# Four experts for each of 32 tokens in one gather of a hybrid decoder's expert mixer

## The chip, the core and the metric

The kernel is one program on one core of a Trainium2 chip. The metric is the time of one execution in device microseconds. Three runs of the kernel before gave 2209.43, 2210.4 and 2212.69 us; the median is 2210.4 us.

## What is computed

Two layers run over 256 prompt tokens and 8 sample tokens of width 1024. Each layer has four recurrent mixers, gates, an output projection and then the expert mixer ("PEER") that the change is about. For every token each of 8 heads picks its best 16 of 16384 experts; an expert is one row of U and one row of V. The reference, cut to that mixer:

```python
def peer_ffn(xn, w_q, keys, U, V):
    ...
    s = jnp.einsum('nhcd,hckd->nhck', q, keys.astype(jnp.float32))
    s1, i1 = lax.top_k(s[:, :, 0], PEER_TOPK)
    s2, i2 = lax.top_k(s[:, :, 1], PEER_TOPK)
    ...
    top, sel = lax.top_k(cand, PEER_TOPK)
    eidx = jnp.take_along_axis(cidx, sel, axis=-1)
    gate = jax.nn.softmax(top, axis=-1)
    ...
        hid = jax.nn.gelu(jnp.einsum('nkd,nd->nk', U[eb], xb).astype(jnp.float32), approximate=False)
        return jnp.einsum('nk,nkd->nd', (hid * gb).astype(xb.dtype), V[eb])
```

So a token has 128 experts (8 heads by 16), and its output is the sum of 128 V rows, each weighted by gelu(U row . xn) times its gate.

## The kernel before, in words

The program is written engine by engine, with semaphores set by hand; each engine works off its own list in order. The change lies in the expert mixer, the second half of each layer.

**Slots.** The 256 prompt tokens stand on the 128 partitions as two halves (tt = 0, 1). Slot s of a half is the s-th expert of every token of it: 128 slots a half, 256 for the prompt, and 8 more slots for the 8 sample tokens, which come just ahead of the last 8 prompt slots. A layer so has 264 slots. The [128, 2048] buffer of a slot holds one U row and one V row for each partition; there are 8 such buffers (`row(k)`), four in `ring` and four in `arena`.

**One slot passes five engines' queues.** GpSimd (POOL) issues an indirect DMA that fetches 128 rows of 8 KB (`fetch`, L1508 to L1517), once the buffer is free (`row_free`). VectorE (DVE) multiplies the U rows by the normalised tokens `xtok` and sums along the row (`dot`, L2076 to L2083), one value a partition. ScalarE (ACT) takes the gelu, multiplies by the gate and scales a pattern of ones to a 128x64 matrix `dg` (`gelu`, L1403 to L1408). TensorE (PE) adds the weighted V rows into PSUM (`weighted`, L1002 to L1009) with four matmuls of 64 rows by 64 columns over 512 elements each, and frees the buffer. A PE matmul in f32 shows as two records in the trace.

**Experts that aren't fetched.** 32 of the 128 first keys are chosen for a layer; the experts of these keys are computed densely by PE, so their rows get an index that is out of bounds, and the gather skips them. The dense work is spread over the slots: up products (`up_products`, L1036) beside slots 0 to 95, the one-hot gates of the dense experts (`gate_slots`, `one_hot`) beside slots 96 to 159, down products (`down_slots`, L1077 to L1091) from slot 168 on.

**Routing.** DVE finds the experts of two heads and a half at a time (`routing`, L1981 to L2064; four groups a half, eight a layer). The first group is done before the first dot, the second beside it, the others are cut into six pieces placed at fixed slots between the dots, up to slot 104. `finish` (L2039 to L2058) ends a group: the indices go to `eidx`, the gates to `gate_w`, each [128 tokens, slots].

**Loads.** The queue of SyncE (SP) loads blocks of dense experts of 512 KB each into four buffers `ub`, in order, each as soon as its buffer is free. **End of a layer.** After the last slot PE closes the sum, ACT copies it out, PE turns it and DVE adds it to the residual `x`, half a bank pair at a time (`sums_out`, `turned`, `add_turned`); then the next layer's norm begins.

## Time and profile before

| what | us |
|---|---|
| median of three runs | 2210.4 |
| the profiled execution: span from its first to its last instruction | 2214.4 |
| PE busy | 2024.7 (91%) |
| DVE busy | 1442.4 (65%) |
| ACT busy | 857.2 (39%) |
| POOL busy | 745.7 (34%) |
| PE, weighted sums (L1007), both kinds of buffer | 290.8 + 291.3 |
| DVE, dots (L2083), both kinds of buffer | 319.7 + 319.8 |

The page gives the profiled execution's span and no other time of it; it is 4.0 us above the median of the runs. "Busy" is time in which an engine executes; matmuls are pipelined, so the records of a full PE overlap. The DMA share is the mean busy share of the core's 16 DMA engines. PEclk is the granted TensorE clock, 1.00 being the upper of its two levels. An idle time stands with the engine or DMA that ended it. L numbers are lines of the kernel.

### The profile page before, as it was taken

The page shows a single profiled execution, that of the slowest core. Times are in us where ns is not written, and L with a number is a line of the kernel's source. Part 1 is how long each engine was busy: PE and PEld are TensorE (multiplying, and loading weights), DVE is VectorE, ACT ScalarE, POOL GpSimd, SP SyncE. Part 2 cuts the span into 40 slices and gives each one's busy share as a digit, 9 for nine tenths or more (in the row PEclk, how much of TensorE's full clock was granted, in tenths as well). Part 3 has the DMA queues.
Part 4 walks back from the last instruction along what each step waited for, and adds up shares of the span by engine and source line. Part 5 has one row for each costly group of instructions (what it writes and reads, how often), then busy time and mean ns, then how long its engine had stood idle before and what let it go on. Part 6 is the DMA issues. An engine that isn't in the chain of part 4 may idle for free.

```text
span 2214.4 us, 37965 instructions
## 1 busy us (share of the span) xinstructions
PE 2024.7 (91%) x13044; PEld 1237.7 (56%) x13044; DVE 1442.4 (65%) x3377; ACT 857.2 (39%) x2476; POOL 745.7 (34%) x658
## 2 busy tenths in 40 slices
PE   7999989989999888999889898899999997789997
PEld 6777668864444222454477776788544442234444
DVE  2425454589999898545533454645899989975545
ACT  2221222144545785433322213221544557853332
POOL 0400000025545676544303000000455456765442
PEclk9999889999999999999999999999999999999999
DMA  6330233568899999999843202437699999999995
GB/s 276 116 116 2 80 110 129 212 236 316 310 349 358 371 358 345 362 372 393 357 186 114 96 5 77 157 123 265 216 320 351 364 365 350 374 375 390 373 381 238
DMA packets 121546, 569.81 MB, mean 257 GB/s; under 512 B 42504, under 2 KB 44712, under 8 KB 61608
## 3 DMA queue, kind: packets, MB, share of 16 engines
q0 software_dynamic: 76032, 389.07, 46.7%
q1 hardware_dynamic: 43648, 175.12, 21.7%
q10 hardware_dynamic: 1696, 3.45, 0.4%
q8 instruction: 94, 1.54, 0.3%
q14 instruction: 76, 0.62, 0.1%
HBM read 725.63 MB, written 6.58 MB: 331 GB/s over the span
## 4 chain that ended last, share of the span: by engine, by line
PE 56%; DVE 24%; issue 10%; ACT 4%; DMA 4%; another core or an unknown queue 1%; POOL 0%; DVEq 0%; SPq 0%; ACTq 0%; POOLq 0%
PE ps L1088 12%; PE ps L1007 10%; PE ps L607 10%; PE ps L672 7%; DVE arena L2083 6%; PE ps L929 3%; PE ps L962 3%; PE ps L943 3%; DMA arena<-in_uv,arena 2%; DVE arena L2108 2%; PE ps L1036 1%; DVE arena L1978 1%; DVE arena L1969 1%; DMA ring<-in_uv,arena 1%; DVE arena L1968 1%
## 5 line engine op out<-in xcount | busy, mean ns | idle before, releaser
L1516 POOL DMA_INDIRECT arena<-in_uv,arena x264 | 332.2, 1258 | 267.6 <-PE ps L1007 214.1
L1516 POOL DMA_INDIRECT ring<-in_uv,arena x264 | 327.1, 1239 | 273.3 <-PE ps L1007 235.3
L2083 DVE SCALAR_TENSOR_TENSOR arena<-arena 128x1024 bf16<-128x1024 f32 x264 | 319.7, 1224 | 117.0 <-DMA arena<-in_uv,arena 110.5
L2083 DVE SCALAR_TENSOR_TENSOR arena<-ring,arena 128x1024 bf16<-128x1024 f32 x264 | 319.8, 1224 | 112.7 <-DMA ring<-in_uv,arena 102.2
L1007 PE MATMUL ps<-arena 64*64 64x512 f32 x2112 | 290.8, 622 | 51.0 <-ACT arena L1408 46.6
L1007 PE MATMUL ps<-ring,arena 64*64 64x512 f32 x2112 | 291.3, 623 | 45.4 <-ACT arena L1408 41.4
L1406 ACT ACTIVATE arena<-arena 128x1 f32<-128x1 f32 x528 | 105.3, 200 | 505.6 <-DVE arena L2083 499.0
L1506 POOL COPY arena<-arena 128x8 uint32 (+1 forms) x66 | 36.2, 548 | 739.2 <-DVEq L2050 738.8
L1088 PEld LDWEIGHTS ps<-hold,ub 128*128 128x128 f32 x1024 | 180.3, 189 | 161.1 <-issue 143.6
L1088 PE MATMUL ps<-hold,ub 128*128 128x256 f32 x1024 | 268.8, 398 | 0.0
L672 PE MATMUL ps<-xn,ring 128*128 128x264 f32 x1024 | 244.9, 398 | 15.1 <-remote 12.9
L672 PEld LDWEIGHTS ps<-xn,ring 128*128 128x128 f32 x1024 | 197.2, 195 | 52.2 <-issue 17.6
L1036 PEld LDWEIGHTS ps<-xn,ub 128*128 128x128 f32 x768 | 135.0, 191 | 134.6 <-issue 122.0
L1036 PE MATMUL ps<-xn,ub 128*128 128x256 f32 x768 | 207.6, 402 | 0.0
L607 PE MATMUL ps<-xn,ring 128*128 128x264 f32 x896 | 205.8, 389 | 0.0
L1408 ACT ACTIVATE arena<-const,arena 128x64 f32<-128x64 f32 x528 | 183.7, 348 | 17.2
L607 PEld LDWEIGHTS ps<-xn,ring 128*128 128x128 f32 x896 | 170.4, 191 | 33.2 <-issue 4.8
L1407 ACT ACTIVATE arena<-arena 128x1 f32<-128x1 f32 x528 | 155.6, 295 | 17.1
L1007 PEld LDWEIGHTS ps<-arena 64*64 64x64 f32 x2112 | 55.7, 132 | 140.6 <-issue 140.6
L1007 PEld LDWEIGHTS ps<-ring,arena 64*64 64x64 f32 x2112 | 56.3, 132 | 131.8 <-issue 131.7
L1190 ACT ACTIVATE arena<-ps 128x264 f32<-128x264 f32 x60 | 23.7, 395 | 206.8 <-PE ps L607 206.6
L1238 ACT ACTIVATE arena<-ps 128x264 f32<-128x264 f32 x50 | 19.3, 390 | 202.2 <-PE ps L672 201.9
(453 smaller groups left out, 2465.4 us busy)
## 6 DMA issues: line engine op xcount, KB each, us to landing
ring<-in_w SPq DMA_DIRECT2D x84, 1024.0 KB
ub<-in_uv SPq DMA_DIRECT2D x64, 512.0 KB
ub<-in_ud SPq DMA_DIRECT2D x48, 512.0 KB
hold<-in_ud SPq DMA_DIRECT2D x16, 512.0 KB, 6.4
ring<-in_uv,arena POOLq DMA_INDIRECT x264
arena<-in_uv,arena POOLq DMA_INDIRECT x264
ub<-in_w SPq DMA_DIRECT2D x4, 1024.0 KB
hold<-in_st SPq DMA_DIRECT2D x2, 2048.0 KB
```

What stands on the lines that cost most here:

```text
L607: m = mm(bank(b), w, xg[:, kt, :] if t < PLAIN_TILES else xn[:, kt, :], start=kt == 0, stop=kt == KT - 1)
L672: m = mm(bank(b), ring[:, j, at:at + P], xn[:, kt, :], start=kt == 0, stop=kt == KT - 1)
L929: m = mm(bank(b), ring[:, j, at:at + P], yy[:, 2 * m_ + k, :], start=k == 0, stop=k == 1)
L943: m = mm(bank(6 + o % 2), ring[:, j, at:at + P], src[:, kt, :], start=kt == 0, stop=kt == KT - 1)
L1007: m = mm(ps[chunk(q ^ half), SUM_BANK[tt] + half, :], dg[chunk(q), k, :], row(k)[chunk(q), D + 512 * half:D + 512 * half + 512], start=Fal ...
L1036: m = mm(bank(4 + j % 4, SEQ), u[:, kt * P:kt * P + P], xn[:, kt, 0:SEQ], start=kt == 0, stop=kt == KT - 1)
L1088: m = mm(bank(4 + dt // 2, SEQ, SEQ * (dt % 2)), ub[:, j % UB, dt * P:dt * P + P], hd[:, j, :], start=False, stop=False, skip_group_check= ...
L1406: own(act(hge[:, k:k + 1], hid[:, k:k + 1], ACT.Gelu))
L1407: own(act(hgg[:, k:k + 1], hge[:, k:k + 1], ACT.Copy, scale=gate))
L1408: act(dg[:, k, :], C("channel"), ACT.Copy, scale=hgg[:, k:k + 1]).then_inc(dg_full[k], 1)
L1516: e.indirect_dma_start(out=row(k), out_offset=None, in_=A["uv"], in_offset=bass.IndirectOffsetOnAxis(ap=ix[:, par, k:k + 1], axis=0), **sk ...
L2083: stt(prod[:, n % 2, :], u, 1.0, xtok[:, tt, :], ALU.mult, ALU.mult, accum_out=hid[:, k:k + 1]).then_inc(S("dve_hid"), 1)
```

## The change

A gather now fetches four experts for each of 32 tokens. Partition 32q + t of a slot holds expert q of token t of the group; a half is cut into four token groups g, a routing group r gives 32 slots: for each g eight, k = 0 to 7, with the ranks k and k + 8 of both heads on the four strips q. The number of slots, buffers, fetched rows and skipped rows stays.

- `dot` reads `rep[:, g]`, the 32 normalised tokens of group g written four times one below the other. SP makes these copies with 16 DMAs inside the chip for each half, 32 partitions by 4 KB each (`copies_of_rows`). `rep` and the spread indices and gates (`lay`) lie over constants that the mixer doesn't need; ACT reloads these at the end of layer 0.
- At the end of a routing group DVE spreads indices and gates with 16 copies of 32 partitions (`by_tokens`), and signals the group to POOL after them; for the first group the indices are spread and signalled first, and the gates in a second set of 16.
- `weighted` multiplies all 128 partitions by a 128x32 matrix, which sums over the four experts; four matmuls, each over 256 of the 1024 columns, go to four strips of 32 PSUM partitions.
- The first half of the second tt's sum is copied out, turned and added before the last 8 slots instead of after them; the sample sum is 256 wide instead of 1024. Loops of PE over slots are written out.

```diff
+TG = 32
+QS = P // TG
...
+        rep = const[:, OVER:OVER + QS * D].rearrange("p (a b) -> p a b", b=D)
+        lay = const[:, OVER + QS * D:OVER + QS * D + TT * 2 * SLOTS].rearrange("p (a b) -> p a b", b=2 * SLOTS)
...
-        dg = carve(SLOT, HD)
+        dg = carve(SLOT, TG)
...
+        def place(s):
+
+            tt, n = divmod(s, P)
+            return tt, n // (QS * SLOT), n // SLOT % QS
...
+                def copies_of_rows(tt):
+
+                    e.wait_ge(S("act_xt"), tt + 1)
+                    for g in range(QS):
+                        if tt:
+                            e.wait_ge(S("dve_hid"), P - (QS - 1 - g) * SLOT)
+                        if tt or g:
+                            e.wait_ge(S("sp_rep"), 16 * QS * (tt * QS + g))
+                        for q in range(QS):
+                            e.dma_start(rep[q * TG:q * TG + TG, g, :], xtok[g * TG:g * TG + TG, tt, :]).then_inc(S("sp_rep"), 16)
...
+                        if j == AHEAD[-1] + 2:
+                            copies_of_rows(0)
...
-                down_blocks(0, 12)
+                down_blocks(0, UB)
+                copies_of_rows(1)
+                down_blocks(UB, 12)
...
-                    for half in range(2):
-                        for q in range(2):
-                            m = mm(ps[chunk(q ^ half), SUM_BANK[tt] + half, :], dg[chunk(q), k, :], row(k)[chunk(q), D + 512 * half:D + 512 * half + 512],
-                                   start=False, stop=False, skip_group_check=True)
+                    for q in range(QS):
+                        m = mm(ps[TG * q:TG * q + TG, b, lo:lo + D // QS], dg[:, k, :], row(k)[:, D + D // QS * q:D + D // QS * (q + 1)],
+                               start=False, stop=False, skip_group_check=True)
...
                         if s == n - SLOT:
+                            close_sum(SUM_BANK[1])
                             e.wait_ge(S("dve_xa"), 1)
...
+                        if s == n - SLOT // 2:
+                            turned(1, 0, 3)
...
+                        sums_out(1, 2, 0)
...
+                if l + 1 < L:
+                    e.dma_start(const[:, OVER:NCONST], A["const"][:, OVER:NCONST]).then_inc(S("act_const"), 16)
+                sums_out(1, 4, 1)
...
+                def by_tokens(n, lo, hi):
+
+                    tt, r = divmod(n - 1, GROUPS)
+                    of = eg[:, tt, lo:hi, r * GH * TOPK:(r + 1) * GH * TOPK]
+                    to = lay[:, tt, :].rearrange("p (r g a k) -> p r g a k", r=GROUPS, g=QS, a=2)[:, r, :, lo:hi, :]
+                    for g in range(QS):
+                        for q in range(QS):
+                            i = e.tensor_copy(to[q * TG:q * TG + TG, g], of[g * TG:g * TG + TG, :, q * SLOT:q * SLOT + SLOT])
+                    own(i)
...
-                            e.sem_inc(S("dve_route"), 1)
+                            own(stt(to_idx, n1, layer_off[0:p1, 0:1], n2, ALU.add, ALU.add))
+                            if n == 1:
+                                by_tokens(n, 0, 1)
+                                e.sem_inc(S("dve_route"), 1)
...
+                            by_tokens(n, int(n == 1), 2)
+                        if n != 1:
                             e.sem_inc(S("dve_route"), 1)
...
-                    of = eidx[:, tt, :].bitcast(U32)
-                    ts(ix_u[:, 0, :], of, 7, 127, ALU.logical_shift_right, ALU.bitwise_and)
+                    of = ix_u[:, 1, :]
+                    own(e.tensor_copy(of, eg[:, tt, 0, :]))
+                    own(ts(ix_u[:, 0, :], of, 7, 127, ALU.logical_shift_right, ALU.bitwise_and))
...
+                    tt, r, g = place(s)
+                    if r == 0 and s % SLOT == 0:
+                        e.wait_ge(S("sp_rep"), 16 * QS * (tt * QS + g + 1))
+                    dot(s % P, rep[:, g, :], s + (SLOT if s >= samples else 0), row_round + s // SLOT)
```

The order of DVE's instructions before, where the second group's routing ends beside slots 4 and 5 (L2039 to L2058 are `finish`, L2083 is the dot):

```order
L2044 SCALAR_TENSOR_TENSOR arena<-arena 128x32
L2048 TENSOR_SCALAR arena<-arena 128x32
L2049 SCALAR_TENSOR_TENSOR arena<-arena,layer_off 128x32
L2052 TENSOR_REDUCE arena<-arena 128x2
L2053 RECIPROCAL arena<-arena 128x2
L2054 TENSOR_TENSOR arena<-arena 128x32
L2056 SCALAR_TENSOR_TENSOR arena<-arena 128x32
L2083 SCALAR_TENSOR_TENSOR arena<-arena 128x1024 x3
```

The same place now (L2025 is `by_tokens`, L2133 the dot):

```order
L2091 SCALAR_TENSOR_TENSOR arena<-arena 128x32
L2095 TENSOR_SCALAR arena<-arena 128x32
L2096 SCALAR_TENSOR_TENSOR arena<-arena,layer_off 128x32
L2101 TENSOR_REDUCE arena<-arena 128x2
L2102 RECIPROCAL arena<-arena 128x2
L2103 TENSOR_TENSOR arena<-arena 128x32
L2105 SCALAR_TENSOR_TENSOR arena<-arena 128x32
L2025 COPY const<-arena 32x16 x16
L2133 SCALAR_TENSOR_TENSOR arena<-arena,const 128x1024 x3
```

Sixteen copies stand between the end of the routing and the next dots; the other six later groups have the same, and the first group has two such rows of 32x8.

The order of PE's instructions before, in the down products (L1007 is `weighted`, L1088 a down product; the ISA rows take a semaphore):

```order
L1007 MATMUL ps<-arena 64x512 x4
L1088 MATMUL ps<-hold,ub 128x256 x3
L411 ISA
L1007 MATMUL ps<-arena 64x512 x4
L411 ISA
L1088 MATMUL ps<-hold,ub 128x256 x3
```

The same stretch now (L1039 is `weighted`, L1123 a down product):

```order
L426 ISA
L1039 MATMUL ps<-ring,arena 32x256 x4
L1123 MATMUL ps<-hold,ub 128x256
L426 ISA
L1123 MATMUL ps<-hold,ub 128x256 x2
L426 ISA
L1039 MATMUL ps<-ring,arena 32x256 x4
```

Nothing moved against the down products; the four matmuls of a slot write 32 partitions by 256 columns instead of 64 by 512.

## Rows read from the trace of the kernel before

**Rows 1.** Windows: stretch, length, busy PE, PEld, DVE, ACT, POOL; PEclk, DMA share, GB/s.

```profile
526.00:730.00 204.00, 193.69 (x1095) 92.66 (x1091) 189.62 (x549) 104.43 (x323) 106.24 (x93) 1.00 0.94 338
730.00:862.00 132.00, 107.58 (x1131) 33.05 (x1131) 124.07 (x205) 102.40 (x319) 92.77 (x75) 0.99 0.95 357
872.00:1098.00 226.00, 224.23 (x1261) 111.19 (x1257) 120.70 (x215) 81.73 (x283) 110.99 (x100) 0.99 0.98 380
1616.00:1812.00 196.00, 185.41 (x1037) 88.44 (x1035) 182.08 (x537) 98.74 (x304) 101.98 (x88) 0.99 0.94 346
1822.00:1955.00 133.00, 107.23 (x1129) 33.32 (x1125) 123.32 (x203) 101.47 (x317) 91.50 (x72) 0.99 0.97 364
1966.00:2190.00 224.00, 222.24 (x1259) 110.88 (x1260) 120.21 (x215) 81.36 (x280) 116.26 (x100) 1.00 0.98 383
```

**Rows 2.** Groups view, DVE, 488 to 730 us: busy, mean ns | idle before, what ended it.

```profile
L2083 DVE SCALAR_TENSOR_TENSOR arena<-ring,arena 128x1024 bf16<-128x1024 f32 x51 | 61.0, 1225 | 3.0 <-DMA ring<-in_uv,arena 0.8 <-DVE arena L2101 0.6 <-DVE arena L2029 0.4
L2083 DVE SCALAR_TENSOR_TENSOR arena<-arena 128x1024 bf16<-128x1024 f32 x48 | 57.2, 1225 | 1.6 <-DVE arena L2029 0.4 <-DVE arena L2101 0.3 <-issue 0.2
...
L2035 DVE TENSOR_TENSOR arena<-arena 128x1024 bf16<-128x1024 bf16 x7 | 4.8, 692 | 5.4 <-ACT arena L1365 4.6 <-issue 0.8
```

**Rows 3.** Groups view, DVE, 730 to 862 us.

```profile
L2083 DVE SCALAR_TENSOR_TENSOR arena<-arena 128x1024 bf16<-128x1024 f32 x33 | 40.1, 1219 | 1.8 <-DMA arena<-in_uv,arena 1.4 <-DVE x L2127 0.2
...
L2115 DVE TENSOR_TENSOR hold<-hold,ps 128x512 f32<-128x512 f32 x16 | 10.9, 680 | 2.8 <-remote 2.8
L2101 DVE TENSOR_TENSOR arena<-picked_f,arena 128x512 f32<-128x512 f32 x14 | 9.6, 687 | 2.0 <-ACTq L411 2.0
```

**Rows 4.** Groups view, DVE, 862 to 1098 us.

```profile
L2083 DVE SCALAR_TENSOR_TENSOR arena<-arena 128x1024 bf16<-128x1024 f32 x49 | 60.0, 1226 | 53.7 <-DMA arena<-in_uv,arena 51.6 <-issue 1.9 <-DVE arena L2054 0.2
```

**Rows 5.** Timeline, PE, second stretch: start, length, instructions in a row [idle before].

```profile
763.90 1.09 PE L1007 MATMUL ps<-ring,arena 64*64 64x512 f32 x8
764.92 0.42 PE L1071 MATMUL ps<-arena 128*32 128x128 f32 x8
765.28 0.66 PE L1060 MATMUL ps<-const,arena 128*128 128x128 f32 x4
```

**Rows 6.** Timeline, PE, third stretch.

```profile
1083.80 1.09 PE L1007 MATMUL ps<-arena 64*64 64x512 f32 x8
1084.82 1.56 PE L1088 MATMUL ps<-hold,ub 128*128 128x256 f32 x6
1086.31 1.09 PE L1007 MATMUL ps<-arena 64*64 64x512 f32 x8
```

**Rows 7.** Windows view of parts of the third stretch of both layers.

```profile
1040.00:1080.00 40.00, 40.00 (x227) 20.37 (x226) 19.45 (x33) 13.53 (x48) 22.12 (x18) 1.00 1.01 404
1060.00:1080.00 20.00, 20.00 (x115) 10.34 (x115) 8.69 (x15) 5.91 (x21) 10.85 (x9) 1.00 1.02 420
2000.00:2040.00 40.00, 40.00 (x225) 20.06 (x224) 21.13 (x35) 14.88 (x53) 22.76 (x19) 1.00 1.00 388
```

**Rows 8.** Timeline, DVE: small copies in the recurrent mixers of layer 0.

```profile
177.23 0.40 DVE L1702 COPY arena<-arena 128x16 f32<-128x16 f32 x4
...
276.35 0.17 DVE L1835 COPY arena<-arena 128x16 f32<-128x16 f32 x1
...
340.21 0.29 DVE L1884 COPY arena<-arena 128x256 f32<-128x256 f32 x1
```

**Rows 9.** Timeline, DVE: the first dot of layer 0.

```profile
486.48 1.23 DVE L2083 SCALAR_TENSOR_TENSOR arena<-ring,arena 128x1024 bf16<-128x1024 f32 x1
```

**Rows 10.** Timeline, ACT: the first half's normalised rows are put out.

```profile
473.09 1.07 ACT L1390 ACTIVATE arena<-ps 128x512 f32<-128x512 f32 x2
```

**Rows 11.** Timeline, ACT: last sums of layer 0, first root of layer 1.

```profile
1113.30 1.09 ACT L1413 ACTIVATE arena<-ps 128x512 f32<-128x512 f32 x2 [5.26 <-PE ps L1016]
...
1125.11 0.48 ACT L1157 ACTIVATE arena<-ps,const 128x264 f32<-128x264 f32 x1 [3.72 <-PE ps L580]
```

**Rows 12.** DMA issues: destination<-source, queue, count, KB, us to landing.

```profile
const<-in_const ACTq DMA_DIRECT2D x1, 2723.0 KB, 12.9
```

More of the change, by code:

```diff
@@ L1131, in _ @@
                         e.wait_ge(S("act_acc"), 4)
-                        for kt in range(KT):
-                            from_ = NS // 2 * (kt // 4)
-                            m = mm(bank(0, NS, NS * kt), xtok[:, 2, kt * P:kt * P + P], C("group")[:, from_:from_ + NS], start=True, stop=True)
+                        for half in range(2):
+                            m = e.transpose(bank(0, P, P * half), xtok[:, 2, P * half:P * half + P], C("ident"))
                         m.then_inc(S("pe_xa"), 1)
-                close_sum(1)
-                for half in range(2):
-                    turned(1, half, 5 + half)
+                close_sum(SUM_BANK[1] + 1)
+                turned(1, 1, 5)
                 e.sem_inc(arrive, 1)
@@ L2074, in _, with dot @@
                     part()
-                def dot(slot, tt, n, nth):
+                def dot(slot, rows, n, nth):
                     k = slot % SLOT
@@ L2181, in _ @@
                         e.sem_inc(S("dve_xa"), 1)
[L2182 removed]
+                    tt, r, g = place(s)
+                    if r == 0 and s % SLOT == 0:
+                        e.wait_ge(S("sp_rep"), 16 * QS * (tt * QS + g + 1))
+                    dot(s % P, rep[:, g, :], s + (SLOT if s >= samples else 0), row_round + s // SLOT)
                 own.clear()
[L2184 to L2187 removed]
+                e.wait_ge(S("pe_xa"), 4)
+                d = x[:, :, SEQ:N].rearrange("p (q h) t -> p q h t", h=2)
+                own(tt_(d, d, bank(0, 2 * P).rearrange("p (h q t) -> p q h t", h=2, t=TG)[:, :, :, 0:NS], ALU.add))
+                add_turned(1, 1, 5)
                 e.sem_inc(arrive, 1)
```

135 lines of the change are left out of this document (66 added, 69 removed).

## Prediction, made before the changed kernel ran

> **What bounds the kernel now.** I read the page for the long groups, then the stretches of the expert mixer, then what each engine waits for in them, and last the instructions of one slot. A slot is one gather of 128 rows, one dot product on VectorE (DVE), three small ScalarE (ACT) steps and one weighted sum on TensorE (PE); a layer has 264. The mixer of layer 0 falls into three stretches, that of layer 1 into the same three [rows 1]. In the first (526 to 730 us; slots 16 to 96, beside up products and the routing of later groups) DVE is busy 189.6 of 204 us, PE 193.7. In the second (730 to 862, one-hot gates) DVE is busy 124.1 of 132 and PE 107.6. In the third (872 to 1098, down products) PE is busy 224.2 of 226, DVE only 120.7, and the DMA engines' share is 0.98.
>
> Busy shares don't tell which engine is the bound; the waits do. In the first stretch the dots of DVE waited 0.8 us for a landing in 240 us [rows 2]: the rows are always there, and the stretch is as long as DVE's own chain of dots and routing. In the second it is nearly the same: 1.4 us for landings, 2.8 and 2.0 us behind PE and ACT [rows 3]. In the third one of the two groups of dots alone waited 51.6 us for landings [rows 4], because the buffers come free only as PE works through its sums. So PE's weighted sum sets the time in the third stretch only, 450 of the 2214.4 us.
>
> **PE's part.** Before, a slot is eight passes of 64x512 (four matmuls, two records each). They take 1.02 us to the next group's start, and eight passes over 128 columns, in the four column strips that the change uses, take 0.36 us (764.92 to 765.28) [rows 5]. A line through the two gives 0.36 + 128 x (0.66 / 384) = 0.58 us for eight passes over 256 columns. Bounds: half of 1.02 is 0.51, twice 0.36 is 0.72; I take 0.58, which saves 0.44 us a slot. In the first two stretches this goes into PE's idle time, since DVE is late there. In the third the slots start 2.51 us apart where six down passes stand between two sums [rows 6], 2.47 over the stretch (of its 1261 PE records 512 are down passes and some 16 others; the rest is 8 for each of 91.6 slots in 226 us); they would come to 2.03.
>
> The gathers and the down blocks would then have to come at 380 x 2.47 / 2.03 = 462 GB/s. No row has that. The busiest rows of the stretch, with a share of 0.99 to 1.01, carry 388 and 404 GB/s, and 420 in 20 us around the eight sample gathers, which skip no row [rows 7]. So what is late next is the DMA, within a few per cent of where PE stands now. I take 388, the row with a share of 1.00 and only ordinary gathers: 226 x (1 - 380/388) = 4.7 us in layer 0 and 224 x (1 - 383/388) = 2.9 in layer 1, together **-7.6**. The ends are 0 and, at 420 GB/s, -21.5 - 19.7 = -41.2.
>
> The Trainium skill, "DMA: Bandwidth & Descriptors", section "Where 436 GB/s comes from", says that for transfers from HBM the HBM side binds, at about 358 GB/s a core. By that rule the third stretch, already above it, could gain nothing, and the sum below would be 25.0 instead of 17.4 us. The rows of 388 and 404 GB/s differ from it, and the rows decide.
>
> **DVE's part.** After each group's routing the indices and gates are spread by 16 copies of 32 partitions, for the first group twice. That is 9 sets, 144 copies, in a layer. Four copies of 16 elements took 0.40 us, one alone takes 0.17 [rows 8]: (0.40 - 0.17) / 3 = 0.077 us apart, and 0.17 - 0.077 = 0.09 more for the wait at a set's end. 144 x 0.077 + 9 x 0.09 = 11.9 us. Two further copies of 128 elements before the indices are turned cost at most 0.29 each (a copy of 256 elements [rows 8]), 0.6 together. So 12.5 us a layer, **+25.0** in all. All of it is on the path: DVE has no wait for data in the first stretch that could cover it [rows 2], and the two sets of the first group stand before the first dot, which starts with no idle time of DVE before it [rows 9]. PE, ACT and the gathers queue behind it, each through the buffers. Lower end: DVE waits 4.6 us a layer for ACT before a decode [rows 2]; if copies fell fully into that, 25.0 - 9.2 = 15.8. Upper end: copies that don't overlap, 144 x 0.17 = 24.5 a layer, +50.
>
> **The copies of the normalised rows.** 32 new DMAs a layer carry 4 MB inside the chip. No row shows their time. The first 16 are issued when ACT has put out the rows at 474.2 [rows 10], behind four expert blocks on SP's queue that have been issued by then; the first four are needed by the first dot at 486.5, later still by the copies above, the next four eight slots on. SP's next block load waits behind them, for a buffer that comes free later anyway. The second 16 are needed from slot 128 and allowed from slot 104, in the second stretch: 2.1 MB at its 357 GB/s [rows 1] would be 5.9 us if nothing hid them. The DMA share of 0.95 there leaves 6.6 us of 132. I take 0; if that cover is gone, +11.7 for both layers. Against it, PE's shorter sum may end the 2.8 and 2.0 us of DVE's waits there [rows 3], -9.6 at most; I take 0 for that too.
>
> **The end of a layer.** Half of the second block's sum is now copied out and added earlier. That takes one of two ACT copies (0.55 of 1.09) and 0.68 us of DVE (one addition over 512 elements [rows 3]) from the end [rows 11], and the last sum is 0.44 shorter. But PE now stops before the fifth sample slot until all eight samples are weighed and copied out, then has four slots of down products left (8 us), which DVE's additions wait for. I take 0, with -3 to +5. The overwritten constants are reloaded behind layer 0's last gate; the first load of 2723 KB landed in 12.9 us [rows 12], and ACT reads its first constant of layer 1 some 12 us after the last copies of the sums begin [rows 11], and the reload is issued ahead of these, so 0; what lands late there is paid in full.
>
> **Sum.** 25.0 - 7.6 = +17.4 us. On the profiled execution, which has a span of 2214.4 us: 2231.8. The runs' median, 2210.4, is 4.0 below the profile, so I forecast **2227.8 us**, 0.8% slower.
>
> **Rivals.** First, the DMA speeds up once PE no longer holds the buffers: more gathers wait at the engines, and the third stretch runs at 420 GB/s. Then 25.0 - 41.2 = -16.2, **2194 us**, faster. It wins from about 404 GB/s over the whole of both third stretches, where 226 x (1 - 380/404) + 224 x (1 - 383/404) = 25.1 us pays for the copies. For it: PE is busy 40.00 of 40.00 us in the rows of 388 and 404, so PE held those rows back. Against it: a share of 0.99 to 1.01 in the same rows, and that 420 is shown only where all rows of a gather are fetched.
>
> By the same page and section of the Trainium skill the fabric allows 435 GB/s; by that figure alone the two stretches would lose 55 us. No row reaches it.
>
> Second, the gathers come less evenly. Of four tokens and all ranks of a head, rather than eight tokens and one rank, more or fewer are skipped at a time, and each dot waits for the slowest part of its gather. If the second and third stretches (132 + 226 + 133 + 224 = 715 us) become 2% longer, +14.3 in place of the gain, with half of the 11.7 for the copies: 25.0 + 14.3 + 5.9 = +45, **2256 us**. For it: DVE's 1.4 us of waiting for landings in the second stretch, at a share of 0.95, leave little room. Against it: PE gives each buffer back 0.44 us sooner.
>
> The Trainium skill's "DMA: Bandwidth & Descriptors", section "The descriptor swizzle", says that one engine serves four neighbouring partitions in each of two strips of 32. Counted so from the reference's expert indices, the fullest engine of eight gathers has 22% more rows than the mean now and 25 to 27% after. No row shows engines apart.
>
> Third, the four strips don't run side by side. Then eight passes cost 8 x 0.25 = 2.0 us (1.49 us for six passes [rows 6]), 1 us more than now, 264 us a layer less PE's idle time of some 30: about 2670 us. Rows 5 speak against it.
>
> **How the numbers follow.** Forecast 0.66, the DMA rival 0.19, the uneven gathers 0.12, strips in sequence 0.03. A measurement here can tell about 0.2% (4.4 us) from none. Faster by more: 0.15 of the first rival and 0.03 of the forecast's edge (cheap copies with 404 GB/s), 0.18. Within: 0.04 of the rival, 0.07 of the forecast, 0.11. Slower: 0.56 + 0.12 + 0.03 = 0.71. The range must reach some way to the first rival and nearly to the second: 2202 to 2252. The forecast's own range is 2215 to 2245.
>
> **What would show it.** Sixteen small copies per group on DVE, about 1.3 us each set; a first stretch longer by some 10 us with DVE still not waiting for landings; PE's eight passes at about 0.58 us and PE no longer full in the third stretch, where it waits for ACT and ACT for DVE's dots; a DMA share near 1 there at 380 to 395 GB/s. A third stretch shorter by over 12 us a layer, or copies that cost under 6 us a layer, would prove me wrong.

## The result, and the profile after

The changed kernel takes 2312.75 us (median of 4 runs, 2302.66 to 2316.96) beside 2211.55 us before (4 runs): 1.0415 times as long, 95% interval 1.0384 to 1.0447. Slower was forecast, but as 2227.8 us in a range of 2202 to 2252; the measured time is some 100 us above the one before, the forecast one was 17. The profiled execution has a span of 2313.1 us, against 2214.4.

The windows view by the same three stretches (length, busy PE, PEld, DVE, ACT, POOL, PEclk, DMA share, GB/s) is what [rows 1] became:

```profile
534.00:749.00 215.00, 172.68 (x1071) 95.56 (x1068) 200.88 (x636) 99.30 (x311) 94.16 (x90) 0.90 0.87 307
749.00:908.00 159.00, 100.42 (x1183) 48.36 (x1185) 138.25 (x234) 107.73 (x342) 102.22 (x83) 0.72 0.97 343
908.00:1124.00 216.00, 177.59 (x1180) 102.42 (x1172) 115.01 (x206) 75.46 (x270) 110.10 (x97) 0.97 0.98 381
1675.00:1889.00 214.00, 167.71 (x1065) 93.24 (x1066) 199.89 (x635) 98.92 (x310) 98.12 (x90) 0.93 0.88 314
1889.00:2052.00 163.00, 101.25 (x1188) 48.88 (x1186) 139.01 (x236) 108.29 (x343) 98.45 (x80) 0.72 0.96 341
2052.00:2270.00 218.00, 178.85 (x1180) 103.18 (x1172) 114.71 (x205) 75.00 (x268) 108.74 (x100) 0.97 0.99 386
```

PE is no longer full in the third stretch (177.6 of 216 us where it was 224.2 of 226), yet the stretch is as long as it was, and the DMA engines carry 381 and 386 GB/s where they carried 380 and 383. The first two stretches are longer. To compare kernels I cut each trace at the starts of dots: dot 0, 96, 168 and 256 of a layer (the third part so holds the eight sample slots), dot 263, the last, and VectorE's MEMSET that ends the recurrent mixers. In us, layer 0 / layer 1:

| part | before | after | grew by |
|---|---|---|---|
| MEMSET to dot 0 | 74.4 / 74.3 | 80.1 / 80.6 | 12.0 |
| dots 0 to 96 | 234.5 / 236.0 | 257.4 / 256.9 | 43.8 |
| dots 96 to 168 | 148.5 / 151.1 | 159.4 / 162.8 | 22.6 |
| dots 168 to 256 | 215.7 / 214.1 | 216.0 / 218.5 | 4.7 |
| dots 256 to 263 | 20.7 / 16.5 | 21.1 / 21.6 | 5.5 |
| last dot of layer 0 to MEMSET of layer 1 | 396.4 | 406.3 | 9.9 |
| start and end of the program | 432.1 | 432.4 | 0.3 |

The sum is 98.8 of the 98.7 us between the two spans. How far a row can be trusted shows in a second profile of the kernel before (told below, under the clock): 74.3 / 74.3, 234.2 / 236.0, 148.0 / 149.3, 217.5 / 216.3, 21.3 / 14.5 and 404.8 us in the first six rows, with a span of 2226.6. Against it the third stretch grew by 0.7 us instead of 4.7, and the mixers by 1.5 instead of 9.9; the three rows ahead of it and the last slots stay as large.

The groups view of VectorE shows what the first stretch holds now (491 to 749 us; it answers to [rows 2]):

```profile
L2133 DVE SCALAR_TENSOR_TENSOR arena<-ring,const 128x1024 bf16<-128x1024 f32 x49 | 58.5, 1224 | 2.4 <-DVE arena L2076 0.7 <-DVE const L2025 0.6 <-DVE arena L2143 0.2
L2133 DVE SCALAR_TENSOR_TENSOR arena<-arena,const 128x1024 bf16<-128x1024 f32 x48 | 57.1, 1222 | 2.1 <-DVE const L2025 0.9 <-DVE arena L2076 0.6 <-DVE arena L2143 0.2
L2025 DVE COPY const<-arena 32x16 f32<-32x16 f32 x112 | 20.9, 186 | 1.6
```

The dots wait for no landing there, as forecast; the 112 copies of seven sets are new, and they are busy 20.9 us with 1.6 us of idle time before them, against 22.9 us by which this part of layer 0 grew. The timeline shows a set of the first group and one of a later group:

```profile
477.34 2.81 DVE L2025 COPY const<-arena 32x8 f32<-32x8 f32 x16
...
620.79 3.07 DVE L2025 COPY const<-arena 32x16 f32<-32x16 f32 x16
```

Sixteen copies take 2.8 to 3.1 us, some 0.175 us apart, where the prediction had 1.3. Cut out of the trace, the 18 sets last 56.0 us together.

In the second stretch (749 to 908 us) the dots now do wait for landings, 8.0 and 5.8 us in the two groups of dots where [rows 3] has 1.4 in one:

```profile
L2133 DVE SCALAR_TENSOR_TENSOR arena<-ring,const 128x1024 bf16<-128x1024 f32 x36 | 44.0, 1223 | 11.5 <-DMA ring<-in_uv,arena 8.0 <-issue 2.0 <-DVE arena L2152 1.3
L2133 DVE SCALAR_TENSOR_TENSOR arena<-arena,const 128x1024 bf16<-128x1024 f32 x36 | 43.9, 1225 | 8.4 <-DMA arena<-in_uv,arena 5.8 <-issue 1.2 <-DVE arena L2152 0.8
```

The DMA view of 765 to 825 us, in 40 slices of 1.5 us, shows when:

```profile
DMA  9999999999989999999999999999999999988899
GB/s 415 361 273 243 249 279 328 421 388 404 421 366 404 415 377 317 273 270 257 292 415 410 410 421 388 366 371 322 276 240 270 260 314 404 410 366 290 328 273 361
```

The share stays at 80% or more, but at regular distances the rate falls from over 400 to 240 to 290 GB/s for 7 to 9 us. These are the row copies of the second half; they are allowed after dots 104, 112, 120 and 128, four at a time. One burst in the windows view, and the same place (behind dot 112) in the kernel without these copies, which is told below:

```profile
787.24:794.46 7.22, 3.60 (x52) 1.90 (x44) 5.59 (x10) 5.49 (x18) 5.63 (x5) 0.77 1.04 285
```

```profile
782.30:789.80 7.50, 5.71 (x75) 2.95 (x73) 7.46 (x14) 6.01 (x20) 5.76 (x5) 0.85 1.00 403
```

In the trace's packets, one gathered row of 8 KB takes 469 ns on average during the four bursts and 341 ns in the rest of the stretch.

PE's eight passes came out as forecast (timeline of the third stretch; 0.56 to 0.57 us to the next group's start, against 0.58), and PE waits for ACT between them:

```profile
1043.02 0.64 PE L1039 MATMUL ps<-ring,arena 128*32 128x256 f32 x8 [0.92 <-ACT arena L1441]
1043.58 1.56 PE L1123 MATMUL ps<-hold,ub 128*128 128x256 f32 x6
```

In the third stretch of layer 0, PE's down products and sums made 96% of the chain that ended last; now the landings of gathers make 68% of it (critical view of 872 to 1098 us before, and of 908 to 1124 us after):

```profile
by line: PE ps L1088 56.2%; PE ps L1007 40.1%; DMA arena<-in_uv,arena 6.7%; issue 0.3%; PE ps L1013 0.1%; POOLq L1516 0.0%; POOLq L411 0.0%; POOLq L1537 0.0%
```

```profile
by line: DMA arena<-in_uv,arena 46.1%; DMA ring<-in_uv,arena 21.7%; issue 10.2%; PE ps L1123 7.8%; PE ps L1039 6.6%; POOL arena L1552 1.7%; ACT arena L1441 1.4%; ACT arena L1440 1.3%; ACT arena L1439 0.9%; PE ps L1045 0.8%; POOL ring L1552 
```

### The profile page after: what moved, and what is told of

Same layout as the page of the kernel before. It is cut to its first block, busy times and chain, and to the rows that moved or that the text cites. A ratio compares the mean times of both kernels' runs of the same rounds, so it can differ in the third digit from the quotient of the medians.

```text
span 2313.1 us, 38254 instructions
## 1 busy us (share of the span) xinstructions
PE 1888.4 (82%) x13016; PEld 1273.8 (55%) x13016; DVE 1497.5 (65%) x3673; ACT 843.5 (36%) x2474; POOL 719.7 (31%) x658
## 4 chain that ended last, share of the span: by engine, by line
PE 21%; DMA 17%; DVE 15%; issue 8%; ACT 3%; POOL 1%; SPq 0%; DVEq 0%; another core or an unknown queue 0%; POOLq 0%; ACTq 0%
DMA arena<-in_uv,arena 10%; DMA ring<-in_uv,arena 7%; PE ps L637 5%; DVE arena L2133 4%; PE ps L702 3%; PE ps L1039 2%; PE ps L1123 2%; PE ps L959 1%; PE ps L992 1%; PE ps L973 1%; DVE const L2025 1%; DVE arena L2015 1%; ACT arena L1441 1%; DVE arena L2006 1%; DVE arena L2005 1%
## 5 line engine op out<-in xcount | busy, mean ns | idle before, releaser
L2133 DVE SCALAR_TENSOR_TENSOR arena<-ring,const 128x1024 bf16<-128x1024 f32 x256 | 310.2, 1225 | 126.4 <-DMA ring<-in_uv,arena 110.7
L2133 DVE SCALAR_TENSOR_TENSOR arena<-arena,const 128x1024 bf16<-128x1024 f32 x256 | 309.6, 1224 | 106.6 <-DMA arena<-in_uv,arena 97.0
L1439 ACT ACTIVATE arena<-arena 128x1 f32<-128x1 f32 x528 | 106.3, 201 | 672.2 <-DVE arena L2133 670.9
L1039 PE MATMUL ps<-ring,arena 128*32 128x256 f32 x2112 | 186.8, 429 | 178.1 <-ACT arena L1441 174.7
L1039 PE MATMUL ps<-arena 128*32 128x256 f32 x2112 | 202.2, 460 | 138.0 <-ACT arena L1441 137.7
L1123 PE MATMUL ps<-hold,ub 128*128 128x256 f32 x1024 | 273.9, 404 | 0.0
L1542 POOL CAST arena<-const 128x8 uint32 (+1 forms) x64 | 31.6, 493 | 754.5 <-DVEq L2099 754.2
L702 PE MATMUL ps<-xn,ring 128*128 128x264 f32 x1024 | 247.6, 401 | 14.4 <-remote 13.1
L1123 PEld LDWEIGHTS ps<-hold,ub 128*128 128x128 f32 x1024 | 183.7, 193 | 92.6 <-issue 74.4
L1039 PEld LDWEIGHTS ps<-ring,arena 128*32 128x32 f32 x2112 | 45.2, 113 | 270.3 <-issue 269.9
L1039 PEld LDWEIGHTS ps<-arena 128*32 128x32 f32 x2112 | 45.8, 117 | 243.0 <-issue 243.0
L1441 ACT ACTIVATE arena<-const,arena 128x32 f32<-128x32 f32 x528 | 169.6, 321 | 17.2
L1440 ACT ACTIVATE arena<-arena,const 128x1 f32<-128x1 f32 x512 | 150.9, 295 | 16.6
```

The costliest lines, as they stand in the source:

```text
L702: m = mm(bank(b), ring[:, j, at:at + P], xn[:, kt, :], start=kt == 0, stop=kt == KT - 1)
L1039: m = mm(ps[TG * q:TG * q + TG, b, lo:lo + D // QS], dg[:, k, :], row(k)[:, D + D // QS * q:D + D // QS * (q + 1)], start=False, stop=Fals ...
L1123: m = mm(bank(4 + dt // 2, SEQ, SEQ * (dt % 2)), ub[:, j % UB, dt * P:dt * P + P], hd[:, j, :], start=False, stop=False, skip_group_check= ...
L1439: own(act(hge[:, k:k + 1], hid[:, k:k + 1], ACT.Gelu))
L1440: own(act(hgg[:, k:k + 1], hge[:, k:k + 1], ACT.Copy, scale=gate))
L1441: act(dg[:, k, :], C(of), ACT.Copy, scale=hgg[:, k:k + 1]).then_inc(dg_full[k], 1)
```

## The experiments

My theory after the result had four parts: **copies** (VectorE's 56 us, all on the path), **row copies** (the second half's 16 take DMA time from the gathers in the second stretch), **the third stretch** stands at the DMA engines, and **the clock** (PE's new idle time lowers it and so costs the recurrent mixers 10 us). The rivals were the buffers, uneven gathers, a faster DMA, and chance. All ratios are to the kernel before on the same chip.

**One copy in place of sixteen.**

```diff
-                    for g in range(QS):
-                        for q in range(QS):
-                            i = e.tensor_copy(to[q * TG:q * TG + TG, g], of[g * TG:g * TG + TG, :, q * SLOT:q * SLOT + SLOT])
-                    own(i)
+                    own(e.tensor_copy(to, of.rearrange("p a (g k) -> p g a k", k=SLOT)))
```

> The 16 copies of a set are replaced by one copy of 128 partitions that leaves indices and gates at their old tokens, so the gathers fetch as many rows, but for other tokens than the dot then takes. Theory of the copies: in the changed kernel's trace the 18 sets take 56.0 us on VectorE, one copy at a time (0.175 us), all on the path; one copy of 0.2 us in place of each set gives back 56.0 - 18 x 0.2 = 52 us, 2313 to about 2261, all of it before slot 96 of the two layers (27 and 25 us). Rival (the buffers or the gathers bind there as well, and VectorE's time turns into waits): under 20 us, above 2293, with VectorE waiting for landings in the first stretch.

Measured: 2263.86 us, ratio 1.0215 (1.018 to 1.0251); span 2260.0, 53 less than the changed kernel's. The starts go back to 74.8 / 74.8 us, dots 0 to 96 to 244.8 / 242.3. That the total meets the forecast 52 is in part luck: 38.3 us of it lie ahead of slot 96, where all 52 were expected, 10.6 in the third stretch, which the expectation left out, and 6.9 in the mixers of layer 1, which vary by as much; other parts took 2.7 back. What is missing ahead of slot 96 was held back by the first half's row copies: with these left out in both kernels (next runs), one copy in place of sixteen gives 50.1 us from the two MEMSETs to dot 96. So nearly all of the 56.0 us was on the path.

**Without row copies.** For the second half alone (the call of `copies_of_rows(1)` and its wait go), for both halves, and for both halves together with the one copy:

> The 16 copies of normalised rows for the second half are left out, and its dots take the rows of the first half. Theory of the row copies: they share the DMA engines with the gathers in slots 104 to 128, where the landing latency went from 7 to 13 or 14 us; slots 96 to 168 lose the 11.0 and 11.6 us that they gained, 2313 to about 2290, and the DMA share of 0.99 there falls back to 0.95. Rival (the new order of tokens and ranks makes the gathers uneven): slots 96 to 168 stay at 142 to 145 us and the time within 5 us of 2313.

> All 32 copies of normalised rows of a layer are left out; the dots take the 128 rows of a half as before the change. Theory of the row copies: as when the second half's are left out, about 2290, since the first 16 run ahead of the first dots and nothing waited for them; the first dot starts within 1 us of where it starts in the changed kernel. Rival (the first 16 delay the first gathers or the block loads): 5 to 10 us less than that, within the first 16 slots of each layer.

> Both are left out: one copy in place of 16, and no copies of normalised rows. If the two costs are separate, 2313 - 52 - 23 = 2238. What is then left over 2211 (about 27 us) is the clock in the recurrent mixers of layer 1 (11 us), the third stretches and the last slots (10), and it doesn't lie in the first two stretches. Rival (with both gone the shorter weighted sum shows at last): the third stretch or the second gets shorter than before the change, and the time falls to 2200 or below.

Measured: 2283.65 us (1.0292, 1.0252 to 1.0332), 2278.83 us (1.0276, 1.0243 to 1.031) and 2230.63 us (1.0049, 1.0028 to 1.007). The windows view of dots 96 to 168 of layer 0 without the second half's copies:

```profile
749.30:895.50 146.20, 98.48 (x1187) 48.05 (x1185) 137.51 (x235) 107.51 (x342) 106.60 (x83) 0.75 0.96 360
```

This part falls from 159.4 / 162.8 to 146.3 / 148.2 us, 27.7 us in all and 2.2 and 2.9 below the kernel before: 2.1 MB a layer cost 13 to 15 us. (Layer 0's 13.1 is the cleaner figure, since these kernels choose other experts in layer 1. The latency in the expectation is read too low: the landings that the changed kernel's trace has at slots 104 to 128 came 14.7 to 16.0 us after their issue.) The granted clock, a mean of time at 2.4 and at 1.2 GHz, is nearly as low here (0.75) as in the changed kernel (0.72), so it isn't the clock that makes the stretch long. The first half's copies cost nothing while the sixteen copies stand ahead of the dots; once these are gone, dots 0 to 96 take 244.8 / 242.3 us with and 237.5 / 237.4 without them, so they would be next. The two costs account for nearly all: what is left is a half per cent, in a kernel whose one copy also leaves the gathers in their old order, which turns out below to be worth some us by itself.

**Which copies overlap.** Seven extra sets ahead of the true ones, each in another form (three of the seven are shown):

```diff
+                        if n == 2:
+                            x_ = e.tensor_copy(to[A_, b], of[A_, :, src])
...
+                        if n == 4:
+                            x_ = e.tensor_copy(to[h, b], of[f, :, sa])
...
+                        if n == 7:
+                            x_ = e.tensor_copy(to[B_, a], of[B_, :, sa])
```

> Ahead of the true set of the routing groups 2 to 8 stands an extra set of copies in another form: group 2 sixteen of 32x16 within their partitions, group 3 four of 128x16, group 4 eight of 64x16 moved by 64 partitions, group 5 sixteen of 32x16 moved, into another tensor, group 6 four of 32x64 moved, group 7 sixteen of 32x16 within their partitions on changing strips, group 8 sixteen of 128x16 into another tensor. Theory (copies that move rows to other partitions don't overlap): the forms of groups 4, 5 and 6 start 0.175 us apart or more, those of 2, 3, 7 and 8 0.077 apart, as the 128x16 copies in the recurrent mixers do. First rival (copies of 32 partitions don't overlap, moved or not): 2 and 7 are 0.175 apart too, 4 lies between. Second rival (it is the target or the pattern): 5 and 8 differ from the rest. The extra copies take 12 to 14 us a layer, and as VectorE's time is on the path there, the time grows by as much as they take, some 2313 + 26.

Measured: 2331.6 us (1.0489, 1.0434 to 1.0543). The timeline of the seven extra sets (start, length, operation, count):

```profile
506.04 1.82 DVE L2031 COPY const<-arena 32x16 f32<-32x16 f32 x16
...
546.88 0.46 DVE L2033 COPY const<-arena 128x16 f32<-128x16 f32 x4
...
585.12 0.82 DVE L2036 COPY const<-arena 64x16 f32<-64x16 f32 x8
...
625.02 3.07 DVE L2038 COPY arena<-arena 32x16 f32<-32x16 f32 x16
...
665.89 1.01 DVE L2040 COPY const<-arena 32x64 f32<-32x64 f32 x4
...
704.90 3.10 DVE L2042 COPY const<-arena 32x16 f32<-32x16 f32 x16
...
745.95 1.33 DVE L2044 COPY arena<-arena 128x16 f32<-128x16 f32 x16
```

All three guesses were wrong. Moving rows isn't it: the 64x16 copies (L2036) move rows by 64 partitions and overlap. Nor are 32 partitions, or the target tensor. L2031 and L2042 are the same unmoved copies; in the first four in a row stay on one strip, in the second each is on another strip than the last, and the first takes 1.82 us, the second 3.10. Copy by copy, starts lie 0.076 to 0.088 us apart while the partitions stay the same and 0.17 us or more where they change. The seven last 11.6 us together, and dots 0 to 96 grew by 11.2 / 11.6: what VectorE does there is paid in full.

**The order of the copies.** Does the source's strip count, or the target's?

```diff
-                    for g in range(QS):
-                        for q in range(QS):
+                    for q in range(QS):
+                        for g in range(QS):
```

> The 16 copies in another order: four with the same target strip one after another, the source strip changing, where before the target changed and the source stayed. Theory (copies overlap when they write the same partitions): 12 of 16 steps fall to 0.077 us, a set from 3.1 to about 1.9 us, 2313 to about 2292. Rival (both source and target must stay the same): 3.1 us as before, 2313.

Measured: the 18 sets last 55.6 us (56.0 before the swap), the span is 2303.9, and dots 0 to 96 take 257.0 / 257.1 us, as in the changed kernel: the 9 us less lie elsewhere (4.2 us ahead of the expert mixer of layer 0, 3.2 in the recurrent mixers of layer 1). The rival holds: a change of either one stops the overlap, and so no order of 16 pairs of strips helps.

**The shorter sum alone.** The kernel before, first with two of the four matmuls, then with four over half of the columns:

```diff
-                    for half in range(2):
+                    for half in range(1):
```

> The kernel before with two of its four weighted matmuls a slot: half of the columns get no sum, PE's eight passes become four, nothing else changes. It is the shorter sum without copies, row copies and other order. Theory (the third stretch stands at the DMA engines): slots 168 to 256 stay at 210 to 218 us in both layers, DVE waits for landings there instead of PE, the first two stretches lose under 5 us, and with PE idler the granted clock falls below 0.95 and the recurrent mixers of layer 1 take 400 us or more where they took 396; in all 2210 to 2230, no faster than before. Rival (freed buffers let the DMA run at 420 GB/s): 20 us less in each third stretch, about 2175.

```diff
-row(k)[chunk(q), D + 512 * half:D + 512 * half + 512],
+row(k)[chunk(q), D + 512 * half:D + 512 * half + 256],
```

> The kernel before with each of the four weighted matmuls of a slot over 256 columns instead of 512: half of the columns get no sum. With two of four matmuls left out the passes took 1.01 us as before, since the four quarters of the array work side by side; by the length of the rows the sum should now take 0.5 us, as in the change. Layer 1 then routes other experts, so layer 0 is read. Theory (the third stretch stands at the DMA engines): slots 168 to 256 of layer 0 take 208 to 217 us (215.7 before), with VectorE waiting for landings and PE no longer full; first stretch 230 to 235, second 145 to 149; the time 2205 to 2230. Rival (420 GB/s): 195 us there, and 2175 in all.

The first was a miss: four passes take as long as eight did (timeline; 1.00 us to the next group's start, [rows 6] had 1.02), since the 64x64 quarters had run side by side. So nothing was relieved, and its 2229.53 us (1.0028, 1.0003 to 1.0052) tell nothing of relief.

```profile
1045.38 1.08 PE L1007 MATMUL ps<-arena 64*64 64x512 f32 x4
1046.38 1.56 PE L1088 MATMUL ps<-hold,ub 128*128 128x256 f32 x6
```

The second took 2204.86 us, ratio 0.9914 (0.9884 to 0.9943), 0.9% faster. As its layer 1 chooses other experts, what the shorter sum gives by itself is read in layer 0. Its third stretch of layer 0 (windows view):

```profile
869.00:1079.00 210.00, 187.65 (x1223) 111.77 (x1224) 114.42 (x205) 77.55 (x268) 115.15 (x99) 0.98 0.99 392
```

Dots 168 to 256 take 210.3 us, 5.4 less than before (7.2 less than in the second profile of before), at 392 GB/s and with PE no longer full; the next bound is the DMA, as forecast with 388. The first two stretches stay, at 234.2 and 148.1 us.

**Why the change did not get these 5 us.** In layer 0, where all of these kernels route alike, dots 168 to 256 take 210.3, 210.6 and 209.9 us in the three kernels that have the shorter sum and the old order of gathers (the one just told, one copy, one copy without row copies), and 216.0 to 218.2 us in the seven, above and below, that have the new order and no further matmuls. The changed kernel and the one with one copy run the same instructions there and differ only in which rows a gather fetches. Two windows of just this part, the first in the old order, the second in the new one (one copy without row copies; no second half's row copies):

```profile
869.00:1079.00 210.00, 176.99 (x1180) 102.16 (x1172) 114.64 (x206) 75.88 (x270) 106.10 (x97) 0.98 0.99 393
```

```profile
895.50:1113.00 217.50, 178.69 (x1180) 102.99 (x1172) 114.66 (x206) 75.82 (x270) 109.89 (x97) 0.97 0.98 378
```

If the cause is that skipped rows fall unevenly, it must go when nothing is skipped. So the dense experts' rows were fetched too, in both orders:

```diff
-                            own(ts(n2, n1, float(EXPERTS), float(SKIP), ALU.is_ge, ALU.mult))
+                            own(ts(n2, n1, float(EXPERTS), -float(EXPERTS), ALU.is_ge, ALU.mult))
```

> The changed kernel with nothing skipped: the rows of the dense experts are fetched too (their gates stay zero), so every gather has 128 rows whatever its order. Only slots 168 to 256 of layer 0 are read, beside the next run. By the bytes (88 x 128 rows of 8 KB and the down blocks, 107 MB at 385 GB/s) they take about 275 us. Theory (the change's third stretch lost 6 us to its order because the skipped rows fall unevenly): the same as in the next run, within 2 us. Rival (something else of the change holds the stretch back): 5 us or more above it.

> The same with one copy in place of 16, which leaves the gathers in the order of before the change (and the sums with other experts than their weights). Theory: slots 168 to 256 of layer 0 as in the run beside it, within 2 us. Rival: 5 us or more below it, as with skipping (209.9 and 210.6 against 216.0 to 218.2).

Measured, in one profile each: 257.3 us in the new order, 257.1 in the old one; the difference is gone. Both are below the 275 that the bytes gave, since the rate rose. The windows of the two, new order first:

```profile
965.00:1220.00 255.00, 181.43 (x1168) 103.16 (x1168) 113.73 (x203) 74.88 (x267) 110.52 (x96) 0.97 1.01 417
```

```profile
960.00:1215.00 255.00, 180.67 (x1168) 102.83 (x1167) 113.67 (x203) 74.93 (x268) 109.17 (x96) 0.98 1.01 417
```

With every gather whole the engines carry 417 GB/s. With skipped rows they carry 390 to 393 in the old order and 378 to 382 in the new one (dots 168 to 256 of layer 0 in each kernel): it is the skipping, and in layer 0 the new order makes it worse. Which engine or which partitions come last can't be seen here; the prediction's own count of the fullest engine (22% above the mean, then 25 to 27%) points the same way. For layer 1 no kernel with the old order and the shorter sum chooses the same experts, and the five with the new order that do take 213.1 to 218.5 us (214.1 and 216.3 in the two profiles of before): no gain there either, but how much of that is the order is not shown.

**The clock.** More matmuls in each slot of the changed kernel, adding a product with zeros, bring PE's work back to what it was:

```diff
+                    for q in range(QS - 1):
+                        mm(ps[TG * q:TG * q + TG, b, lo:lo + D // QS], nothing[:, 0:TG], row(k)[:, D + D // QS * q:D + D // QS * (q + 1)],
+                           start=False, stop=False, skip_group_check=True)
```

> The changed kernel with three more matmuls a slot, of the same shape, that add a product with zeros: PE's work per slot is what it was before the change (1.02 us). Theory (PE's idle time lowers the granted clock, and the clock costs the recurrent mixers of layer 1 their 10 us): the mean clock goes from 0.906 to 0.97 or more, the mixers of layer 1 from 406 to 396 us, the time to about 2303, though PE has more to do. Rival (the clock there falls by chance or for another reason, 399 to 406 us in five runs): they stay at 400 to 406, and the time stays at 2313 or grows.

> The kernel without the second half's row copies (its dots take the first half's rows), with the three matmuls with zeros of the run before that kept PE as busy as before the change. One more sample of the clock: theory (PE's idle time in the slots lowers the clock in layer 1's recurrent mixers later): 395 to 397 us there, where the same kernel without the matmuls took 403.7. Rival (chance): 399 to 406.

> The kernel before, unchanged, for a second profile. Theory of the clock: layer 1's recurrent mixers take 395 to 398 us again (396.4). Rival (chance): 399 to 406, as in the changed kernels.

Measured: 2311.56 us (1.0416, 1.0362 to 1.047), no gain; the mean granted clock rose from 0.906 to 0.961 and the recurrent mixers of layer 1 took 395.2 us, just as the theory had it. But the second sample took 404.0 at a mean clock of 0.965, and the kernel before, profiled again, 404.8 (span 2226.6). Over all 17 profiles this part takes 395.2 to 406.3 us; the kernel before lies near both ends of that. These are its two profiles:

```profile
1105.90:1502.30 396.40, 362.75 (x2434) 296.53 (x2431) 187.81 (x409) 93.40 (x191) 25.05 (x30) 0.97 0.31 109
```

```profile
1106.60:1511.40 404.80, 373.20 (x2438) 303.73 (x2439) 187.88 (x409) 93.38 (x191) 25.04 (x30) 0.94 0.30 107
```

The work is the same, and the time goes with the clock granted in this part itself: 0.97 in the two shortest of the 17 (395.2 and 396.4 us), 0.94 to 0.95 in all from 402.6 us up. What fell is the theory that PE's idle time in the slots decides it, since the unchanged kernel shows both levels of time. Why a run gets one or the other stays open, and nothing shows these 10 us as an effect of the change. So some 89 us of the 98.7 are the change's own in these two profiles; against the second profile of before, whose mixers took 404.8 us, the whole difference is 86.5 us.

**A mended change.** ScalarE makes the copies, and PE turns the early half of the second sum after the last down products:

```diff
+                            i = act(to[q * TG:q * TG + TG, g], of[g * TG:g * TG + TG, :, q * SLOT:q * SLOT + SLOT], ACT.Copy)
...
-                        if s == n - SLOT // 2:
-                            turned(1, 0, 3)
...
+                turned(1, 0, 3)
                 close_sum(SUM_BANK[2])
```

> ScalarE makes the 16 copies in place of VectorE, one set for the first group too, and signals GpSimd; and PE turns the early half of the second sum after the last down products instead of ahead of the last four slots of them. Theory of the copies: VectorE's 56.0 us go, ScalarE has the room (half idle in the first stretch), and the first stretches and the starts fall to what one copy in place of sixteen gave, 46 to 52 us less. Theory of the turn: the last eight slots of layer 1 fall from 21.6 to about 16.5 us, those of layer 0 stay. Together 2313 - 50 - 5 = 2258. Rival: the copies hold up ScalarE's three steps a slot by 3 us each time, and half of the gain is lost, 2285.

Then also, for the second half, one row copy at a time:

```diff
+                            if tt and q:
+                                e.wait_ge(S("dve_hid"), P - (QS - 1 - g) * SLOT + 2 * q)
```

> The changed kernel with the copies on ScalarE and the late turn of the early half, and the second half's row copies issued one by one, two slots apart, instead of four at a time. Theory (the copies cost the DMA engines' time wherever it is taken, since the gathers fill them): slots 96 to 168 of layer 0 stay at 160 us, 2271 in all. Rival (it is the burst that makes the gathers late): 152 us or less there, in all 2255 or less, still slower than the kernel before.

Measured: 2271.14 us (1.0234, 1.0183 to 1.0286), where 2258 was expected, and 2268.44 us (1.0216, 1.0171 to 1.0262). Dots 0 to 96 fall to 236.2 / 236.1 us, so ScalarE had the room, but the start grew to 84.3 / 82.8: its one set ahead of the first gather takes 3.56 us (timeline of ACT) and comes after its own work, at 482.92, where VectorE had begun at 473.5.

```profile
482.92 3.56 ACT L1450 ACTIVATE const<-arena 32x16 f32<-32x16 f32 x16
```

The late turn took 21.1 / 21.6 us for dots 256 to 263 to 18.4 / 14.7, below the kernel before (20.7 / 16.5 and 21.3 / 14.5). The changed kernel's own rows show what it removed: PE stands still until ACT has put out the early half, and VectorE, in its turn, until PE has gone through four more slots of down products (timelines of PE and DVE, layer 1).

```profile
2270.99 1.12 PE L1054 MATMUL ps<-const,arena 128*128 128x128 f32 x4 [8.15 <-ACT arena L1445]
```

```profile
2282.31 0.69 DVE L2183 TENSOR_TENSOR x<-x,ps 128x512 f32<-128x512 f32 x1 [8.15 <-PE ps L1159]
```

Single row copies changed nothing: dots 96 to 168 take 162.1 / 164.6 us, so it is the engines' time and not the burst. No version of the change came out below the kernel before.

## Why the prediction was wrong

**The copies, +25.0 forecast, 56 measured.** This is the step that failed most, a term of the sum that was sized wrongly. The count, the place and "all of it is on the path" were right; the price wasn't. "Four copies of 16 elements took 0.40 us" [rows 8] was read as the price of any chain of small copies, but those four are on the same 128 partitions, and the sixteen change theirs at each step. The upper end, 0.17 each and +50, was in the text as the price of "copies that don't overlap"; the row for one copy alone was the nearer one. The range didn't even reach to the stated ends: with +50, +11.7 for the row copies, nothing gained in the third stretch and +5 at the ends of the layers it would have gone to 2277 us instead of 2252, and the measured time lies beyond that too. The Trainium skill, "VectorE: DVE Perf Modes", section "Two Vector instructions with no wait between them", says that an instruction whose input or output starts in another group of 32 partitions than that of the instruction before is held until all earlier ones have finished. The runs agree, with 0.076 to 0.088 us where partitions stay and 0.17 or more where they change; by that rule every one of the sixteen would have been priced like the copy alone in [rows 8].

**The row copies, 0 forecast, 28 measured for the second half.** "The DMA share of 0.95 there leaves 6.6 us of 132" was taken for cover. It was none: the gathers of this stretch were just fast enough for DVE, any time taken from them came out as waits, and 2.1 MB took 13 to 15 us a layer, not the 5.9 that the stretch's own rate gives, since the rate falls to 240 to 290 GB/s while they run. The stated end, +11.7 for both layers, was less than half of it. Against it stand 5 us by which the stretch is shorter than before once these copies are gone. I had 0 for a gain from the shorter sum there, with an end of -9.6; that the 5 us are this gain is not shown, since the kernel before with the shorter sum takes 148.1 us in layer 0, and without it 148.5 and 148.0.

**The third stretch, -7.6 forecast, +4.7 measured** (+0.7 against the second profile of before). The mechanism was right: PE's sum took 0.57 us, PE stopped being the bound, and the DMA came next. With the sum alone the stretch of layer 0 lost 5.4 us, where the forecast had 4.7. What failed is the step from that to the change: the second rival (the gathers come less evenly) was weighed against the forecast as if only one of them could be. Both hold: the new order costs the third stretch about 6 to 8 us in layer 0, and the gain is gone; in layer 1 the gain is missing too, the share of the order in that being open. In the second stretch, where that rival also had 2%, no loss from it can be seen (146.3 and 148.2 us without row copies).

**The first rival** (420 GB/s) fell. "420 is shown only where all rows of a gather are fetched", which stood against it, was the very reason: 417 GB/s come when nothing is skipped. By the Trainium skill, "DMA: Bandwidth & Descriptors", section "Where 436 GB/s comes from", some 358 GB/s would be the end for transfers from HBM; 417 over 255 us differ from it, and the measurement decides. **The third** (strips in sequence) fell with the 0.57 us.

**The end of a layer, 0 forecast with -3 to +5, 5.5 measured** (6.9 against the second profile). That PE would stop and VectorE wait for four slots of down products was said; its price lay just above the stated end.

**The recurrent mixers, not in the sum, +9.9** between these two profiles. No run shows this as an effect of the change; a span that rests on one profile carries it.

With the copies at 56, the row copies at 28 less 5, the third stretch at 4.7 and the end at 5.5, the sum is 89 us, 2303 on a profile of 2214. Of the 72 us by which the forecast missed that, 31 are one row read too widely and 23 a cover that wasn't one (less those 5 us).

## What to carry to other kernels

Price a chain of small VectorE instructions by a row that touches the same partitions from one to the next as the new one will; where strips changed, each cost its full time here. Where dots stood just at the end of their landings, a DMA share of 0.95 covered nothing: price new transfers at what they take from the gathers. And before rows or tokens are regrouped, ask whether a gather that skips rows still loads the DMA evenly, since its rate may decide as soon as an engine gets faster.

## What the runs showed of the hardware

- Four 64x64 matmuls on the quarters of the array take as long as two, 1.02 and 1.00 us for 512 columns; over 256 columns the four take 0.59 (1043.35 to 1043.94 in the kernel before with the shorter sum).
- VectorE copies of 16 elements start 0.077 us apart on the same partitions, moved by 64 partitions or not, and 0.17 apart or more when source or target strip changes.
- Row copies inside the chip pull the DMA engines' rate from about 400 to 240 to 290 GB/s at an unchanged busy share (285 at 1.04 in one burst, 403 at 1.00 in the same place without them).
- Gathers of 128 whole rows run at 417 GB/s; with some 31% of the rows skipped (23,465 of 33,792 fetched in layer 0) the same stretch runs at 378 to 393, depending on which rows.
- The same recurrent mixers take 395 to 406 us from one profile to the next, at a granted clock of 0.97 to 0.94; in the unchanged kernel 396.4 at 0.97 and 404.8 at 0.94.
